# Post norms of a transformer kernel: odd feature tiles on GpSimd, all tiles singly, squares summed in the second unit

## The chip, the cores and the metric

The kernel runs on one core of a Trainium2 chip. The core has TensorE (PE, matrix products, with its weight loads as PEld), VectorE (DVE), ScalarE (ACT), GpSimd (POOL) and SyncE (SP), which issues the weight loads. Each engine works through its own instructions in order and waits on semaphores for the others. The metric is the device time of one execution in microseconds, the median of several runs. The profile is one more execution, recorded by the hardware profiler; its span is the time from its first to its last instruction.

## The reference

Two transformer blocks in fp32 on 256 tokens of width 1024; before the second block 16 learned tokens are put in front (272 tokens). The first block (sparse attention, latent attention, two MLPs) is not touched. The second one:

```python
def rmsnorm(x, g):
    y = xf * lax.rsqrt(jnp.mean(xf * xf, axis=-1, keepdims=True) + EPS)
    return y * g
for i in range(DEPTH):                                   # DEPTH = 2
    f = swiglu(rmsnorm(h, ffn_norm_pre[i, 0]), w1, w3, w2)
    h = h + 0.5 * rmsnorm(f, ffn_norm_post[i, 0])
    hn = rmsnorm(h, mix_norm_pre[i])
    m = causal_multiscale_pool(hn, ...) if i % 2 == 0 else diff_attention(hn, ...)
    h = h + rmsnorm(m, mix_norm_post[i])
    f = swiglu(rmsnorm(h, ffn_norm_pre[i, 1]), w1, w3, w2)
    h = h + 0.5 * rmsnorm(f, ffn_norm_post[i, 1])
```

So the state h is rebuilt six times as h + norm(f) * gain, and the next norm and product start from it. The change concerns five of these: those that lead into the pool mixer, ffn1, ffn2, the qkv product of the attention, and ffn3. The sixth, at the kernel's end, is done in another way.

## The kernel before, in words

Everything is kept with features on the partitions: the state `X` (`x_state`) is 8 tiles of 128 features by 272 tokens (256 in the last one), `F` (`mixer_out`) holds the output of the product before it, already times its gain. Every product is done as three products of fp32r parts: a high part (`XH`, `xg_high`, made by ScalarE as state times gain) and a low part (`XL`, `xg_low`, the rest, made by VectorE); the weights are split the same way in chunks of 128 x 2048 (`split`: ScalarE copies `w_raw` to `w_high`, VectorE subtracts into `w_low`). A large product is a sequence of units; a unit uses one chunk, 8 feature tiles, two output tiles, 3 matmuls each: 48 matmuls into one of two accumulators `acc`. Unit j needs the low part of chunk j, and that `acc` was evacuated after unit j-2. The norm's factor 1/rms is applied to the output, so unit 0 can run before the sum of squares is known.

At a seam into the next product the order is written out by hand:

- PE sums the squares of `F` over the partitions with a matrix of ones (`sum_with_last`), ScalarE takes log and exp for a first guess of 1/rms (`root`), VectorE makes the variance and three Newton steps (`variance`, `refine`, `newton`; the result is `rstd`).
- VectorE's `post_norm` multiplies `F` by `rstd` into `ta` (`evac_a`) and adds it to `X`, in groups `FINE`: tiles 0, 1, 2-3, 4-5, 6-7; behind each it makes the low parts of the group before.
- ScalarE's `xg` makes the high parts of each group and squares each pair of tiles.
- PE's `up` first runs 5 idle products of 512 columns (`keep_busy`, line 562), then unit 0, tile by tile as the groups come (`xg_waits(FINE)`), with further idle products behind tiles 0 and 1 and the squares of tiles 0 to 3 summed directly from `squares` (`sum_tiles`, line 600); VectorE folds tiles 4 to 7 into `square_sum` (`squares_after`, `fold_squares`), which PE adds behind unit 0 (`sum_rest`, line 607).
- Then ScalarE's `root` for the new norm, `rstd` again, VectorE's evacuation of unit 0 (line 1909), and the split of the third chunk on both engines. The second chunk was split before the seam (`ahead`), except for ffn1, where it is split in the seam.
- At the pool mixer PE runs four pieces of two feature tiles each instead of units, then the sum of squares per token; VectorE folds all eight squares.

GpSimd does little: two constant tables, copies of rope parts in the first block (lines 505 and 510), two tables for the last attention (lines 515 and 516).

## Time and profile before

| | us |
|---|---|
| median of 3 runs | 1645.82 |
| lowest, highest | 1645.07, 1648.28 |
| span of the profiled execution | 1639.2 |
| PE busy | 1596.5 (97%) |
| PEld busy | 1522.2 (93%) |
| VectorE busy | 1011.4 (62%) |
| ScalarE busy | 763.7 (47%) |
| GpSimd busy | 22.7 (1%) |

The profiled execution is given by its span alone; the runs' time also holds what lies around the span. Busy times are averages over the whole kernel; a busy PE includes the idle products of line 562. A timeline row has the start from the span's start, the duration, engine, line, operation, output<-input, shape, a count where several are merged, and in brackets the idle time before it and what ended it. The engines overlap the end of one operation with the start of the next one, so starts may be closer together than the durations.

### The profile page before, as it was taken

How to read it: one execution, taken by the hardware profiler on the slowest of the kernel's cores; microseconds unless marked ns; L12 is line 12 of the kernel's file. 1: busy time of each engine (PE TensorE's matmuls, PEld its weight loads, DVE VectorE, ACT ScalarE, POOL GpSimd, SP SyncE). 2: the span in 40 equal slices, each digit the busy share in tenths (PEclk: the TensorE clock that was granted, in tenths of full speed). 3: DMA queues.
4: the chain of work that ended last, by engine and by line, in shares of the span. 5: the costliest groups of instructions: out<-in, count | busy, mean ns of one | idle time of the engine just before them, and what ended most of it. 6: DMA issues, size and time to landing. Idle time of an engine off the chain costs nothing.

```text
span 1639.2 us, 31001 instructions
## 1 busy us (share of the span) xinstructions
PE 1596.5 (97%) x12665; PEld 1522.2 (93%) x12665; DVE 1011.4 (62%) x1239; ACT 763.7 (47%) x1004; POOL 22.7 (1%) x40
## 2 busy tenths in 40 slices
PE   7989999998999999999999999999999999999999
PEld 5969999998999998999978999989999898889998
DVE  7786665567666546565457665466664656676653
ACT  4345554447555435434445444344443435654443
POOL 0000000013000000000000000000000000000000
PEclk9999999999999999999999999999999999999999
DMA  6701566644266665556622556635567352246673
GB/s 165 184 27 56 180 200 182 196 142 122 78 180 197 188 185 167 176 163 198 183 77 87 174 178 200 182 103 180 179 188 194 102 184 78 78 129 190 194 212 96
DMA packets 347111, 253.03 MB, mean 154 GB/s; under 512 B 32622, under 2 KB 345868, under 8 KB 347036
## 3 DMA queue, kind: packets, MB, share of 16 engines
q1 hardware_dynamic: 345424, 250.00, 51.8%
q10 hardware_dynamic: 1612, 1.97, 0.4%
q8 instruction: 54, 0.88, 0.2%
q14 instruction: 21, 0.17, 0.0%
HBM read 250.90 MB, written 1.05 MB: 154 GB/s over the span
## 4 chain that ended last, share of the span: by engine, by line
PE 86%; DVE 8%; ACT 3%; DMA 2%; issue 1%; SPq 0%; ACTq 0%; DVEq 0%
PE acc L537 25%; PE acc L539 25%; PE acc L538 25%; DVE w_low L1682 2%; ACT w_high L1194 1%; PE acc L562 1%; PE spare L735 1%; PE acc L767 1%; DMA w_raw<-in_ffn_w_dram 1%; PE spare L562 1%; PE acc L753 1%; DVE x_state L1892 1%; DVE xg_low L1726 1%; DVE evac_a L1890 1%; PE acc L1089 1%
## 5 line engine op out<-in xcount | busy, mean ns | idle before, releaser
L1682 DVE TENSOR_TENSOR w_low<-w_raw,w_high 128x2048 fp32r<-128x2048 f32 (+2 forms) x222 | 528.7, 2381 | 379.4 <-ACT w_high L1194 379.4
L1194 ACT ACTIVATE w_high<-w_raw 128x2048 fp32r<-128x2048 f32 (+2 forms) x222 | 441.4, 1988 | 612.9 <-PE acc L539 580.2
L537 PE MATMUL acc<-xg_high,w_high 128*128 128x272 f32 (+2 forms) x2320 | 663.3, 286 | 8.1 <-DVE xg_low L1726 4.4
L538 PE MATMUL acc<-xg_low,w_high 128*128 128x272 f32 (+2 forms) x2320 | 654.6, 282 | 0.0
L539 PE MATMUL acc<-xg_high,w_low 128*128 128x272 f32 (+2 forms) x2320 | 654.6, 282 | 0.0
L537 PEld LDWEIGHTS acc<-xg_high,w_high 128*128 128x128 f32 (+1 forms) x2320 | 435.4, 188 | 20.0 <-issue 9.3
L538 PEld LDWEIGHTS acc<-xg_low,w_high 128*128 128x128 f32 (+1 forms) x2320 | 435.4, 188 | 2.4 <-issue 1.7
L539 PEld LDWEIGHTS acc<-xg_high,w_low 128*128 128x128 f32 (+1 forms) x2320 | 435.4, 188 | 0.2
L537 PE MATMUL acc<-hidden_high,w_high 128*128 128x256 f32 (+1 forms) x1216 | 342.4, 282 | 2.8 <-DVE w_low L1682 2.8
L539 PE MATMUL acc<-hidden_high,w_low 128*128 128x256 f32 (+1 forms) x1216 | 341.7, 281 | 0.0
L538 PE MATMUL acc<-hidden_low,w_high 128*128 128x256 f32 (+1 forms) x1216 | 341.7, 281 | 0.0
L537 PEld LDWEIGHTS acc<-hidden_high,w_high 128*128 128x128 f32 x1216 | 228.8, 188 | 3.8 <-DVE w_low L1682 2.0
L539 PEld LDWEIGHTS acc<-hidden_high,w_low 128*128 128x128 f32 x1216 | 228.8, 188 | 0.0
L538 PEld LDWEIGHTS acc<-hidden_low,w_high 128*128 128x128 f32 x1216 | 228.6, 188 | 0.0
L1909 DVE TENSOR_TENSOR evac_a<-acc,rstd 128x544 f32<-128x544 f32 (+1 forms) x44 | 31.5, 716 | 38.9 <-PE acc L539 38.8
L1917 DVE TENSOR_TENSOR evac_b<-acc,evac_a 128x544 f32<-128x544 f32 (+1 forms) x44 | 31.5, 716 | 35.4 <-PE acc L539 35.0
L562 PE MATMUL spare<-constants,ones 128*128 128x512 f32 (+1 forms) x120 | 49.5, 546 | 1.0 <-DMA constants<-in_constants_dram 1.0
L1199 ACT ACTIVATE xg_high<-x_state,gains 128x272 fp32r<-128x272 f32 (+1 forms) x72 | 33.6, 507 | 28.1 <-DVE x_state L1892 20.9
L562 PEld LDWEIGHTS spare<-constants,ones 128*128 128x128 f32 x120 | 22.0, 194 | 18.5 <-issue 16.4
L537 PE MATMUL acc<-out_high,w_high 128*128 128x256 f32 x128 | 36.3, 283 | 0.5 <-DVE out_low L2015 0.5
L539 PE MATMUL acc<-out_high,w_low 128*128 128x256 f32 x128 | 36.1, 282 | 0.0
L538 PE MATMUL acc<-out_low,w_high 128*128 128x256 f32 x128 | 35.7, 279 | 0.0
(296 smaller groups left out, 1448.2 us busy)
## 6 DMA issues: line engine op xcount, KB each, us to landing
w_raw<-in_ffn_w_dram SPq DMA_DIRECT2D x88, 1024.0 KB, 5.3
w_raw<-in_ffn_w_dram SPq DMA_DIRECT2D x32, 1408.0 KB, 7.0
w_raw<-in_mlp_w_up_dram SPq DMA_DIRECT2D x32, 1024.0 KB, 5.7
w_raw<-in_mlp_w_down_dram SPq DMA_DIRECT2D x32, 1024.0 KB, 5.6
w_raw<-in_attn_w_qkv_dram SPq DMA_DIRECT2D x12, 1024.0 KB, 5.1
w_raw<-in_a_w_in_dram SPq DMA_DIRECT2D x18, 256.0 KB, 4.3
w_raw<-in_a_w_in_dram SPq DMA_DIRECT2D x4, 1024.0 KB, 8.0
w_raw<-in_a_w_out_dram SPq DMA_DIRECT2D x4, 1024.0 KB, 5.1
```

The lines of the kernel that those rows point to most:

```text
L537: pe.matmul(dst, high_w, high, start=first, stop=False)
L538: pe.matmul(dst, high_w, low, start=False, stop=False)
L539: return pe.matmul(dst, low_w, high, start=False, stop=last)
L562: pe.matmul(bank[:, 0:width], ones[:], cst[:, 0:width], start=True, stop=True)
L735: ins = pe.matmul(sp[p % 2][:, c, 0:k.shape[1]], q, k, start=True, stop=not masked(p))
L753: ins = pe.transpose(acc[0][0:nk, p % 2, slot * P:(slot + 1) * P], Pr[p % 2][:, c, k0:k0 + nk], ident)
L767: ins = pe.matmul(acc[1][:, p % 2, c * w:(c + 1) * w], PT[p % 2][0:nk, slot, :], v, start=first, stop=last)
L1194: act.activation(whi[slot(c)][:, 0:SIZES[c]], raw[c % 2][:, 0:SIZES[c]], ACT.Copy).then_inc(S["w_high"], 1)
L1199: ins = act.activation(XH[:, k, 0:T], src[:, k, T0:T0 + T], ACT.Identity, scale=gain[:, gcol + k:gcol + k + 1])
L1682: dve.tensor_tensor(wlo[slot(c)][:, s], raw[c % 2][:, s], whi[slot(c)][:, s].bitcast(F32), ALU.subtract)\
L1909: dve.tensor_tensor(z, acc[(g.u0 + j) % 2][:, :, 0:T], across(rstd[:, 0:T], 2), ALU.mult)\
L1917: dve.tensor_tensor(a, acc[(g.u0 + j + 1) % 2][:, :, 0:T], q, ALU.mult).then_inc(S["dve_evac"], 1)
```

## The change

Five things are changed together, at all five seams.

1. `post_norm` goes tile by tile. VectorE multiplies and adds the even tiles 0, 2, 4, 6; GpSimd (`post_norm_odd`) multiplies and adds the odd tiles 1, 3, 5, 7, in the scratch `tb` (`evac_b`), once `rstd` is ready (`post_rstd`), and signals each with `x_pooled`. VectorE still makes all the low parts.
2. ScalarE (`xg_posted`) makes the high part of each tile singly; the squares of tiles 0-1 and 2-3 follow tiles 2 and 4, those of 4-5 and 6-7 come at the end. PE waits for every tile singly.
3. Unit 0 has no idle products between its tiles and no sums of squares. VectorE folds all eight squares by pairs (`fold_by_pairs`), and PE sums the result in the second unit, behind its second tile (`sum_in_second`). ffn0 stays as it was.
4. The third chunk is split before the root of the new norm, on ScalarE and on VectorE; before, it came after.
5. At ffn1 the second chunk's high part is copied by GpSimd, after pool's product, and VectorE subtracts it before the post norm.

```diff
+            def post_norm_odd(layer, T0, T):
+                pool.wait_ge(S["post_rstd"], layer + 1)
+                for q, k in enumerate(range(1, KD, 2)):
+                    t = tb[q % 2][:, 0, 0:T]
+                    pool.tensor_tensor(t, F[:, k, T0:T0 + T], rstd[:, 0:T], ALU.mult).then_inc(S["pool_step"], 1)
+                    pool.wait_ge(S["pool_step"], 4 * layer + q + 1)
+                    x = X[:, k, T0:T0 + T]
+                    pool.tensor_tensor(x, x, t, ALU.add).then_inc(S["x_pooled"], 1)
+            post_norm_odd(0, 0, T2)
+            c = G["ffn_up1"].c0 + 1
+            pool.wait_ge(S[f"w_landed{c % 2}"], LANDED[c])
+            pool.wait_ge(S["w_used"], c - 1)
+            pool.wait_ge(S["w_high"], c)
+            pool.tensor_copy(whi[slot(c)][:, 0:SIZES[c]], raw[c % 2][:, 0:SIZES[c]]).then_inc(S["w_high"], 1)
+            for layer in range(1, 4):
+                post_norm_odd(layer, 0, T2)
...
+            post_norm_odd(4, META, SEQ)
...
+            def sum_in_second(T):
+                def beside(k):
+                    if k == 1:
+                        sum_squares(T, 1)
+                return beside
...
-                wide(g, 0, T0, T, xg_waits(groups), beside=None if norm_sum else sum_tiles(T))
-                if norm_sum is None:
+                wide(g, 0, T0, T, xg_waits(groups), beside=sum_tiles(T) if by_tile else None)
+                if by_tile:
                     sum_rest(T)
                 begin(g)
-                wide(g, 1, T0, T, between=norm_sum)
+                wide(g, 1, T0, T, between=norm_sum, beside=None if norm_sum or by_tile else sum_in_second(T))
...
-                up(G[f"ffn_up{i}"], T0, T, FINE, KF2 // 2, 5)
+                up(G[f"ffn_up{i}"], T0, T, SINGLES if i else FINE, KF2 // 2, 5, by_tile=i == 0)
...
-                pe.wait_ge(S["xg_ready"], n.add("xg_ready", 1 if q else 2))
+                pe.wait_ge(S["xg_ready"], n.add("xg_ready", 2))
...
+            def xg_posted(gcol, T0, T):
+                for k in range(KD):
+                    sem_ = "x_pooled" if k % 2 else "x_ready"
+                    act.wait_ge(S[sem_], n.add(sem_))
+                    high_parts(k, k + 1, gcol, T0, T, X)
+                    if k in (2, 4):
+                        make_squares(k - 2, k, T0, T, D, X)
+                for k in (4, 6):
+                    make_squares(k, k + 2, T0, T, D, X)
+                n.add("squares")
...
-                    if first:
+                    if first and i == 0:
                         root(T)
                     split(g.c0 + j + 2, it, 2)
+                    if first and i:
+                        root(T)
...
             root(T2)
-            split(G["ffn_up1"].c0 + 1)
-            xg(PRE + KD, 0, T2)
+            xg_posted(PRE + KD, 0, T2)
...
+                product(0)
+                into_state(0)
+                product(2)
+                low_parts(0, 1, gcol, T0, T)
+                into_state(2)
+                low_parts(1, 2, gcol, T0, T)
+                low_parts(2, 3, gcol, T0, T)
+                for k in (4, 6):
+                    product(k)
+                    into_state(k)
+                    low_parts(k - 1, k, gcol, T0, T)
+                    low_parts(k, k + 1, gcol, T0, T)
+                low_parts(KD - 1, KD, gcol, T0, T)
+            def fold_by_pairs(T):
+                dve.wait_ge(S["sq_made"], n.add("sq_made"))
+                for a in (2, 4, 6):
+                    dve.wait_ge(S["sq_made"], n.add("sq_made"))
+                    link(dve.tensor_tensor(squares[:, 0:2, 0:T], squares[:, 0:2, 0:T], squares[:, a:a + 2, 0:T], ALU.add))
+                dve.tensor_tensor(sqsum[:, 0:T], squares[:, 0, 0:T], squares[:, 1, 0:T], ALU.add).then_inc(S["sq_read"], 1)
...
+                    if first and i:
+                        split(g.c0 + j + 2)
                     if first:
                         variance(T)
                         refine(rstd, T)
...
+            split(G["ffn_up1"].c0 + 1)
             variance(T2)
-            refine(rstd, T2)
+            refine(rstd, T2, "post_rstd")
             post_norm(0, T2, gcol=PRE + KD)
-            squares_after(G["ffn_up1"].c0 + 1, T2)
+            fold_by_pairs(T2)
```

VectorE at the seam into ffn2, from the first multiply by `rstd` to the first chunk's split in the new product, before (`evac_a` is the scratch, `w_low_54` the third chunk's low part):

```order
L1890 TENSOR_TENSOR evac_a_74<-mixer_out,rstd 128x544
L1892 TENSOR_TENSOR x_state<-x_state,evac_a_74 128x544
L1726 SCALAR_TENSOR_TENSOR xg_low<-x_state,gains,xg_high 128x272 x4
L1711 TENSOR_TENSOR squares<-squares 128x544
L1714 TENSOR_TENSOR square_sum<-squares 128x272
L1748 TENSOR_SCALAR variance<-spare 128x272
L1756 SCALAR_TENSOR_TENSOR rstd_step<-rstd_guess,variance 128x272
L1757 TENSOR_TENSOR rstd_step<-rstd_step,rstd_guess 128x272
L1758 SCALAR_TENSOR_TENSOR rstd<-rstd_step,rstd_guess 128x272
L1909 TENSOR_TENSOR evac_a_74<-acc,rstd 128x544
L1682 TENSOR_TENSOR w_low_54<-w_raw_50,w_high_52 128x2048
```

And the same place now:

```order
L1935 TENSOR_TENSOR x_state<-x_state,evac_a_75 128x272
L1768 SCALAR_TENSOR_TENSOR xg_low<-x_state,gains,xg_high 128x272 x3
L1957 TENSOR_TENSOR squares<-squares 128x544 x3
L1958 TENSOR_TENSOR square_sum<-squares 128x272
L1724 TENSOR_TENSOR w_low_54<-w_raw_50,w_high_52 128x2048
L1790 TENSOR_SCALAR variance<-spare 128x272
L1798 SCALAR_TENSOR_TENSOR rstd_step<-rstd_guess,variance 128x272
L1799 TENSOR_TENSOR rstd_step<-rstd_step,rstd_guess 128x272
L1800 SCALAR_TENSOR_TENSOR rstd<-rstd_step,rstd_guess 128x272
L1973 TENSOR_TENSOR evac_a_74<-acc,rstd 128x544
```

The fold has four additions instead of two, and the third chunk's subtraction moved from behind the evacuation to ahead of the variance.

ScalarE at the same seam, before (`w_high_52` is the third chunk's high part):

```order
L1205 ACTIVATE squares<-x_state 128x544
L1199 ACTIVATE xg_high<-x_state,gains 128x272 x2
L1205 ACTIVATE squares<-x_state 128x544
L1236 ACTIVATE rstd_guess<-spare,epsilon 128x272
L1238 ACTIVATE rstd_guess<-rstd_guess 128x272
L1194 ACTIVATE w_high_52<-w_raw_50 128x2048
```

And now:

```order
L1227 ACTIVATE xg_high<-x_state,gains 128x272 x3
L1233 ACTIVATE squares<-x_state 128x544 x2
L1222 ACTIVATE w_high_52<-w_raw_50 128x2048
L1276 ACTIVATE rstd_guess<-spare,epsilon 128x272
L1278 ACTIVATE rstd_guess<-rstd_guess 128x272
```

Two squares stand together at the end, and the third chunk moved ahead of the two steps of the root.

## Rows read from the trace of the kernel before

**Rows 1.** The page's part 4: shares of the chain by engine.

```profile
PE 86%; DVE 8%; ACT 3%; DMA 2%; issue 1%; SPq 0%; ACTq 0%; DVEq 0%
```

**Rows 2.** VectorE's timeline at ffn2's seam: start, us, what, count [idle before].

```profile
1081.99 0.44 DVE L1890 TENSOR_TENSOR evac_a<-mixer_out,rstd 128x272 f32<-128x272 f32 x1
...
1090.64 0.91 DVE L1726 SCALAR_TENSOR_TENSOR xg_low<-x_state,gains,xg_high 128x272 fp32r<-128x272 f32 x2 [0.24 <-ACT xg_high L1199]
1091.47 0.72 DVE L1711 TENSOR_TENSOR squares<-squares 128x544 f32<-128x544 f32 x1
...
1095.81 0.44 DVE L1748 TENSOR_SCALAR variance<-spare 128x272 f32<-128x272 f32 x1 [3.14 <-ACT rstd_guess L1236]
...
1097.78 0.72 DVE L1909 TENSOR_TENSOR evac_a<-acc,rstd 128x544 f32<-128x544 f32 x1
1098.42 2.28 DVE L1682 TENSOR_TENSOR w_low<-w_raw,w_high 128x2048 fp32r<-128x2048 f32 x1
```

**Rows 3.** ScalarE's timeline at the same seam.

```profile
1082.94 0.52 ACT L1199 ACTIVATE xg_high<-x_state,gains 128x272 fp32r<-128x272 f32 x1 [2.48 <-DVE x_state L1892]
...
1090.44 0.64 ACT L1205 ACTIVATE squares<-x_state 128x544 f32<-128x544 f32 x1
...
1096.14 1.90 ACT L1194 ACTIVATE w_high<-w_raw 128x2048 fp32r<-128x2048 f32 x1
```

**Rows 4.** PE there: first two rows from the chain, then its timeline.

```profile
1089.98 0.92 PE spare L600 x4
...
1094.79 0.46 PE spare L607 x2
...
1094.89 0.49 PE L537 MATMUL acc<-xg_high,w_high_ahead 128*128 128x272 f32 x1
...
1101.11 0.29 PE L537 MATMUL acc<-xg_high,w_high 128*128 128x272 f32 x1
```

**Rows 5.** GpSimd's timeline in the first block's second attention.

```profile
366.12 0.39 POOL L505 COPY b_k<-b_k 32x256 f32<-32x256 f32 x1
366.46 0.58 POOL L505 COPY b_k<-b_k 32x256 f32<-32x256 f32 x1
```

**Rows 6.** VectorE there; GpSimd's copies begin at 364.39.

```profile
363.04 0.42 DVE L1776 TENSOR_TENSOR evac_b<-evac_a,cos_b 96x256 f32<-96x256 f32 x1
...
370.32 0.61 DVE L1776 TENSOR_TENSOR evac_b<-evac_a,cos_b 128x256 f32<-128x256 f32 x1
370.85 0.41 DVE L1777 TENSOR_TENSOR evac_b<-spare,sin_b 128x256 f32<-128x256 f32 x1
```

**Rows 7.** GpSimd's timeline in the qkv product.

```profile
1305.42 2.19 POOL L515 CAST c_identity<-constants 128x128 fp32r<-128x128 f32 x1 [919.04 <-DVE c_q L2281]
1307.56 0.28 POOL L516 CAST c_mask<-constants 128x128 fp32r<-128x128 f32 x1
```

**Rows 8.** VectorE there.

```profile
1305.18 2.28 DVE L1682 TENSOR_TENSOR w_low<-w_raw,w_high 128x2048 fp32r<-128x2048 f32 x1
```

**Rows 9.** PE's timeline at pool's product: its start, and behind its end.

```profile
846.60 0.36 PE L1017 MATMUL acc<-w_high,xg_high 128*128 128x256 f32 x1 [2.33 <-DVE xg_low L1726]
...
856.37 0.72 PE L1026 MATMUL spare<-ones,square_sum 128*128 128x1 f32 x6
```

**Rows 10.** VectorE at pool's seam, and ahead of ffn1's post norm.

```profile
842.50 0.44 DVE L1890 TENSOR_TENSOR evac_a<-mixer_out,rstd 128x272 f32<-128x272 f32 x1
...
857.74 0.16 DVE L1756 SCALAR_TENSOR_TENSOR tokens_step<-tokens_guess,tokens_variance 128x3 f32<-128x3 f32 x1 [0.15 <-ACT tokens_guess L1361]
...
873.33 0.44 DVE L1748 TENSOR_SCALAR variance<-spare 128x272 f32<-128x272 f32 x1 [2.10 <-ACT rstd_guess L1236]
```

**Rows 11.** Windows: length, busy (x count) by engine, then PEclk, DMA, GB/s.

```profile
390.00:391.00 1.00, 0.00 (x0) 0.00 (x0) 1.00 (x1) 0.99 (x3) 0.00 (x0) 1.00 0.00 0
392.00:393.00 1.00, 1.00 (x6) 1.00 (x5) 0.31 (x1) 0.14 (x1) 0.00 (x0) 0.50 0.03 10
...
840.00:848.00 8.00, 5.67 (x22) 2.96 (x22) 7.13 (x15) 4.10 (x9) 0.00 (x0) 1.00 0.00 0
```

More of the change, by code:

```diff
@@ L1571, in _ @@
             root(T2)
-            split(G["ffn_up1"].c0 + 1)
-            xg(PRE + KD, 0, T2)
+            xg_posted(PRE + KD, 0, T2)
             ffn(1, 0, T2)
-            xg(PRE + 2 * KD, 0, T2)
+            xg_posted(PRE + 2 * KD, 0, T2)
             ffn(2, 0, T2)
-            xg(GAIN["mix_norm_pre_2"] + KD, 0, T2)
+            xg_posted(GAIN["mix_norm_pre_2"] + KD, 0, T2)
             g = G["qkv"]
+            split(g.c0 + 2)
             root(T2)
-            for j in range(11):
+            for j in range(1, 11):
                 split(g.c0 + j + 2)
@@ L1649, in _ @@
             root(SEQ)
[L1650 removed]
+            xg_posted(PRE + 3 * KD, META, SEQ)
             ffn(3, META, SEQ)
@@ L1910, in pair @@
                         .then_inc(S["dve_evac"], 1)
-                    split(g.c0 + j + 2, it, 2)
+                    if not first or not i:
+                        split(g.c0 + j + 2, it, 2)
                     dve.wait_ge(S["gate_silu"], at(ge0 + j // 2 + 1, it, 1))
@@ L1962, in ffn @@
                     variance(T)
-                    refine(rstd, T)
+                    refine(rstd, T, "post_rstd")
                     post_norm(T0, T, gcol=gcol)
```

46 lines of the change are left out of this document (22 added, 24 removed).

## The prediction

> **What bounds the kernel now.** I read the page's chain by engine first [rows 1]: PE holds 86% of it and VectorE 8%, so time can only be won or lost where PE waits. The change sits at five such places, the seams where a post norm rebuilds the state before the next large product: into pool, ffn1, ffn2, qkv and ffn3. I call R the start of the first multiply by the post norm's `rstd`. I took the seam into ffn2, R = 1081.99 [rows 2], as the pattern and read it engine by engine; the others have the same rows.
>
> PE begins unit 1 at 1094.89, R+12.9, and unit 2 at 1101.11: 6.2 for a unit of eight tiles, 0.78 a tile [rows 4]. Unit 0 ends at 12.9 because it holds, beside its own 6.2, two sums of two squared tiles (0.92 each) and one of `square_sum` (0.46) [rows 4], small fillers, and waits for `xg_low`. VectorE needs until 1090.64 + 0.91, R+9.5, for products, additions and low parts [rows 2]. Unit 2, at R+19.1, needs two things of VectorE: the evacuation of unit 0 (1097.78 + 0.72 = 1098.50) and the low part of its chunk (1098.42 + 2.28 = 1100.70) [rows 2]. The second comes last, with 0.3 to 0.4 to spare: unit 1 ends at that same moment. So two deadlines count, the end of unit 0 and the start of unit 2.
>
> **What a GpSimd operation costs.** No GpSimd tensor_tensor is in the trace. Nearest: a cast of 128 columns 0.28 [rows 7], a copy of 256 columns 0.39 [rows 5], so 0.17 plus 0.86 ns per column, 0.41 for 272 columns with one input. With two inputs I double the column part: 0.64. From above: the same copy beside VectorE took 0.58 [rows 5]; doubling its column part (0.41) gives 0.82 + 0.17, about 1.0. I take the middle of 0.41 and 1.0, 0.70, because it lies next to the doubled copy.
>
> **Who shares with whom.** While GpSimd copied, a VectorE multiplication with both inputs in SBUF took 0.61 where the same line took 0.42 before GpSimd had begun; the next one, with an input in PSUM, stayed at 0.41 [rows 6]. The copy itself went from 0.39 to 0.58 [rows 5]. A GpSimd cast of 128 columns that takes 0.28 alone took 2.19 when it met a VectorE subtraction of 2.28 in progress [rows 7, 8]. I read this as turns: one of them moves data, then the other. Products, additions, low parts and folds of the new seam all have two SBUF inputs, so GpSimd's work is not beside VectorE's, it alternates with it.
> The Trainium skill says this outright (SBUF — State Buffer, section Who interferes with whom): a VectorE instruction with two SBUF inputs contends with a GpSimd one that reads SBUF, and the second to issue is blocked. By that rule, the trace agrees: 2.19 against 0.28.
>
> **The change at the seam into ffn2, with turns.** A GpSimd operation and its turn of VectorE take 0.70 + 0.19 (0.58 less 0.39) = 0.89. Eight of them start at R+0.3: odd tiles are in the state at about 2.0, 3.8, 5.6 and 7.4. VectorE gets eight operations in between, the last the product of tile 4. Behind that stand in a row: addition of tile 4 (0.3 to R+7.7), its high part on ScalarE (0.52 [rows 3]), the low parts 3 and 4 (to 8.8), product and addition of tile 6 (2 x 0.44, R+9.7), high parts 6 and 7 (0.94), low part 7 (0.5): R+11.2, against 9.5 before. PE waits for each tile singly, has 0.78 per tile, and no sums in unit 0 any more (two pairs, 1.84, and the last, 0.46, are gone from it). So unit 0 ends 0.2 for PE to see the last low part and one tile (0.8) behind it, R+12.2, 0.7 earlier than before.
> That 0.7 is spent at the next deadline. Unit 1 now holds the sum (0.46): 12.2 + 6.2 + 0.46 = R+18.9. The squares of tiles 4 to 7 (0.64 each pair [rows 3]) end at R+11.9; the fold, three additions of 0.72 [rows 2] with 0.03 between and one of 0.44, ends at R+13.85, just when PE asks for it, two tiles into unit 1 (12.2 + 1.6). Unlike before, the third chunk's split stands ahead of the root: ScalarE's high part waits for unit 0's end, 12.3 + 1.90 [rows 3] = 14.2; VectorE's subtraction 2.28 to 16.6; then variance and Newton steps, 1095.81 to 1097.78, 1.97 [rows 2], and the evacuation 0.72: R+19.3, unit 2 at R+19.4. Queued behind that subtraction on VectorE is the whole root, and PE waits for it. Before: R+19.1. Loss: 0.3. Later units have slack: per pair of units, 12.4 of PE, VectorE has two subtractions of 2.28 and four operations of 0.72, 7.4.
>
> **The other seams.** qkv and ffn3 have the same order (ffn3 with 256 columns): 0.3 each. ffn1: 0.3, and one more: its second chunk's subtraction (2.28) now stands before `variance`, in an idle time of 2.10 [rows 10]: 0.2 more, 0.5. Its high part goes to GpSimd: 2048 x 0.86 ns + 0.17 = 1.9, which begins when pool's product ends.
> Pool, R = 842.50 [rows 10]: PE starts at 846.60 and works through four pieces with fillers until 856.37, 2.44 each [rows 9]; it waits only for the first. Pieces wait for pairs: low part 1 comes at R+5.0, low part 3 at R+8.1; from there 0.2 + 3 x 2.44 puts the end at R+15.6 against 13.9: 1.7. Then GpSimd's cast of 1.9 starts at the moment where VectorE's three-column Newton step stands 1.3 later [rows 10]; by turns that step waits for the rest, 0.6, and PE with it. And PE is idle before the first piece for 2.33 + (5.2 - 4.1) = 3.4 instead of 2.33 [rows 9]. At 390 to 391 PE did nothing, and at 392 the granted clock was 0.50, the 1.2 GHz level [rows 11]; a first piece (2.1 of work) at that level costs what it doubles less the 1.0 that it would wait anyway, about 1. I take 0.4, since before the 2.33 left the clock at 1.00 [rows 11]. Pool: 2.7.
>
> **Sum.** 2.7 + 0.5 + 3 x 0.3 = 4.1 us over the profiled 1639.2. That execution is given by its span alone; it lies 6.6 below the median of the runs, 1645.82, and I carry the difference over: **1649.9**. PE's clock elsewhere, the DMA queue and SP's waits are untouched: SP waits for `w_low`, which comes no later than before except by these amounts.
> At the ends of the price: with 0.41 the turns are 0.60, the last low part is at R+8.9 and unit 2 about 1.7 early at four seams: 4 x -1.7, pool -0.4, cast +0.3, ffn1 +0.2, 1639. With 1.0: +3.0 at four seams, pool +5.7: 1664.
>
> **Rivals.**
> 1. No turns worth the name (GpSimd's two-input form holds VectorE back little). Then VectorE's own 16 operations of 0.36 to 0.44 with their waits end at R+7.8, PE is bound by itself: unit 1 at R+9.1, unit 2 at R+16.2, 2.9 early at four seams, pool 1.9 early; minus 13: **1632.5**. For it: the work halves on paper. Against: [rows 6 to 8].
> 2. Turns, with a dearer operation: 0.80, still between the 0.64 and the 1.0 of the rows, gives turns of 0.99, unit 2 at +1.0 and pool at +3.4: **1653.5**. The Trainium skill (GPSIMD Engine Reference, section Elementwise — side-by-side cycle accounting) has 4497 ns for 2048 fp32 columns, 2.2 ns per column; an estimate from it is 0.77 for 272, and no run here shows it. By that figure the sum would be near this rival's.
> 3. PE's clock. Unit 0 loses its fillers; with bursts of 0.9 and waits of 0.4 to 1.5, if the level fell to 1.2 GHz at each seam as in [rows 11], a unit 0 that is half waiting loses about 1 to 2: **1657**. Decides: whether PE's rest between tiles counts as idle. Against: 2.33 of idle at pool, more than any wait here, left the level at 1.00 [rows 9, 11].
> 4. The gain of unit 0 is real but late work takes it all and no more: **1646**.
>
> **How the numbers follow.** Turns with 0.6 to 0.9: 0.50, of which 0.15 within 0.2% (3.3 us, about what a measurement of this kernel can tell) and 0.35 slower. Turns with a cheaper operation: 0.15 (faster 0.10, same 0.05). No turns: 0.18, faster. Clock: 0.07, slower. Dearer than 0.9: 0.06, slower. No effect: 0.04. Faster 0.28, same 0.24, slower 0.48. The range leaves out half of the no-turn case and the last of the dear one: 1634 to 1660.
>
> **What would show it.** GpSimd's tensor_tensor at 0.7 or more beside VectorE, and VectorE's 0.44 operations printed at 0.6 to 0.9 until R+7.4; unit 1's first matmul near R+12.3, unit 2's near R+19.4 with an idle time ended by `evac_a`. I am wrong if VectorE's operations stay at 0.44 while GpSimd works, if the first matmul of unit 1 comes before R+10.5, or if the granted clock leaves 1.00 in a unit 0.

## The result, and the profile after

| | median us | runs |
|---|---|---|
| before | 1644.71 (1638.98 to 1648.37) | 16 |
| after | 1650.53 (1643.63 to 1661.49) | 16 |

The ratio is 1.0049, 95% interval 1.0034 to 1.0064 (it is not the quotient of the two medians, which differ by 5.8 us only). 0.49% of 1644.71 is 8 us, where the prediction had 4.1 us (0.25%) and a time of 1649.9. The profiled execution of after spans 1650.7, that of before 1639.2.

The page of after, chain by engine, answers [rows 1]: PE gave two points, one to VectorE and one to ScalarE.

```profile
PE 84%; DVE 9%; ACT 4%; DMA 2%; issue 1%; SPq 0%; ACTq 0%; DVEq 0%
```

GpSimd's timeline of after at ffn2's seam (R = 1085.03 here): start, us, what [idle before]. The rows left out alternate in the same way.

```profile
1085.08 1.01 POOL L521 TENSOR_TENSOR evac_b<-mixer_out,rstd 128x272 f32<-128x272 f32 x1 [199.98 <-DVE rstd L1800]
1086.17 0.84 POOL L524 TENSOR_TENSOR x_state<-x_state,evac_b 128x272 f32<-128x272 f32 x1
...
1091.68 0.85 POOL L524 TENSOR_TENSOR x_state<-x_state,evac_b 128x272 f32<-128x272 f32 x1
```

VectorE's timeline there answers [rows 2].

```profile
1085.03 0.44 DVE L1931 TENSOR_TENSOR evac_a<-mixer_out,rstd 128x272 f32<-128x272 f32 x1
1085.51 0.88 DVE L1935 TENSOR_TENSOR x_state<-x_state,evac_a 128x272 f32<-128x272 f32 x1
1086.31 0.99 DVE L1931 TENSOR_TENSOR evac_a<-mixer_out,rstd 128x272 f32<-128x272 f32 x1
...
1094.67 0.49 DVE L1768 SCALAR_TENSOR_TENSOR xg_low<-x_state,gains,xg_high 128x272 fp32r<-128x272 f32 x1
1095.34 0.91 DVE L1768 SCALAR_TENSOR_TENSOR xg_low<-x_state,gains,xg_high 128x272 fp32r<-128x272 f32 x2 [0.18 <-ACT xg_high L1227]
...
1098.44 0.44 DVE L1958 TENSOR_TENSOR square_sum<-squares 128x272 f32<-128x272 f32 x1
1099.76 2.29 DVE L1724 TENSOR_TENSOR w_low<-w_raw,w_high 128x2048 fp32r<-128x2048 f32 x1 [0.87 <-ACT w_high L1222]
1101.97 0.43 DVE L1790 TENSOR_SCALAR variance<-spare 128x272 f32<-128x272 f32 x1
...
1103.86 0.72 DVE L1973 TENSOR_TENSOR evac_a<-acc,rstd 128x544 f32<-128x544 f32 x1
```

ScalarE's timeline there, one row of it, answers the last of [rows 3].

```profile
1097.81 1.92 ACT L1222 ACTIVATE w_high<-w_raw 128x2048 fp32r<-128x2048 f32 x1 [0.99 <-PE acc L560]
```

PE's timeline there, the first multiplies of units 1 and 2, answers the last two of [rows 4].

```profile
1097.55 0.28 PE L558 MATMUL acc<-xg_high,w_high_ahead 128*128 128x272 f32 x1
...
1104.73 0.36 PE L558 MATMUL acc<-xg_high,w_high 128*128 128x272 f32 x1 [0.55 <-DVE evac_a L1973]
```

Eight GpSimd operations of 0.84 to 1.01 take until R+7.5, and every VectorE operation beside them that was 0.44 (0.49 for a low part) is printed at 0.88 to 1.00; the first one, which GpSimd joins at its start, is still 0.44, and those that start behind R+7.5 are at 0.43 to 0.50 again. The last low part ends at 1095.34 + 0.91 = R+11.22 against R+9.56, `square_sum` at R+13.85 against R+10.67. Unit 1 nevertheless starts earlier, R+12.52 against 12.90, as it has no sums ahead of it. Unit 2 starts later, R+19.70 against 19.12, released by `evac_a`: that is the loss. Each seam by itself, from the same rows of the two traces:

| us from R, before / after | last low part | unit 1 | unit 2 | loss |
|---|---|---|---|---|
| ffn1 | 9.56 / 11.22 | 13.02 / 12.51 | 19.03 / 19.69 | 0.66 |
| ffn2 | 9.56 / 11.22 | 12.90 / 12.52 | 19.12 / 19.70 | 0.58 |
| qkv | 9.56 / 11.22 | 12.91 / 12.51 | 19.13 / 19.66 | 0.53 |
| ffn3 | 9.17 / 10.71 | 12.25 / 11.85 | 18.19 / 18.93 | 0.74 |
| pool | 9.55 / 11.22 | | product's end 13.87 / 17.75 | 3.88 |

At the pool the product of after shows two things [rows 9 to 11] did not have. PE's timeline of after, first multiply and the row behind the product, then the windows (length, busy by engine, then PEclk, DMA, GB/s):

```profile
845.44 0.55 PE L1046 MATMUL acc<-w_high,xg_high 128*128 128x256 f32 x1 [3.39 <-DVE xg_low L1768]
...
858.02 0.72 PE L1055 MATMUL spare<-ones,square_sum 128*128 128x1 f32 x6
```

```profile
840.00:848.00 8.00, 4.61 (x17) 3.16 (x16) 7.86 (x11) 2.52 (x5) 7.04 (x8) 0.80 0.00 1
848.00:856.00 8.00, 8.00 (x51) 7.04 (x51) 5.62 (x12) 5.32 (x8) 0.00 (x0) 0.78 0.01 2
```

The granted clock averages 0.80 and 0.78 over these two windows: for 6.8 us, from 0.7 before the first multiply on, it was at 0.50, the 1.2 GHz level. PE's multiplies there are printed at 0.41, where before had 0.28 behind the first one. The second thing is GpSimd's cast. GpSimd's row and VectorE's row beside it, each from its own timeline:

```profile
858.31 1.89 POOL L531 CAST w_high<-w_raw 128x2048 fp32r<-128x2048 f32 x1 [10.54 <-PE spare L1048]
```

```profile
859.39 0.82 DVE L1798 SCALAR_TENSOR_TENSOR tokens_step<-tokens_guess,tokens_variance 128x3 f32<-128x3 f32 x1 [0.15 <-ACT tokens_guess L1403]
```

The three-column step takes 0.82 where it took 0.16 [rows 10]: it ends when the cast ends (859.39 + 0.82 and 858.31 + 1.89 are both 860.2). From the pool's end to ffn1's R it is 19.58 instead of 18.92.

Sum of the seams in this execution, with the 0.66 between the pool and ffn1: 0.66 + 0.58 + 0.53 + 0.74 + 3.88 + 0.66 = 7.05. The two profiled executions differ by 11.5, though. After was 2.2 ahead when it came to the pool's R (840.27 against 842.50), before anything that was changed, and lost 7.0 more than qkv's 0.53 between the R of qkv and that of ffn3. Most of that is at the end of the last attention, where nothing was changed. Windows of after, then of before:

```profile
1408.00:1416.00 8.00, 8.00 (x26) 6.21 (x26) 3.32 (x12) 2.67 (x12) 0.00 (x0) 0.50 0.00 0
```

```profile
1408.00:1416.00 8.00, 7.49 (x45) 5.47 (x46) 5.08 (x13) 6.06 (x13) 0.00 (x0) 1.00 0.01 2
```

From qkv's R to ffn3's R after took 159.94, before 152.41, 7.5 more. It is not all clock: 0.53 is the seam of qkv, about 1.5 a slower pace of qkv's units at full clock (6.08 each instead of 5.92, see the last section), 0.7 a longer wait of PE at R-3.6 of ffn3 (1.57 instead of 0.85) for squares that ScalarE makes behind a weight split, which itself waited for its transfer. That leaves about 4.8 for the fall. Whether it is the change's is taken up in experiment 9.

### The profile page after: what moved, and what is told of

The parts are those of the page before. It is cut to its first block, busy times and chain, and to the rows that moved or that the text cites. A ratio compares the mean times of both kernels' runs of the same rounds, so it can differ in the third digit from the quotient of the medians.

```text
span 1650.7 us, 30945 instructions
## 1 busy us (share of the span) xinstructions
PE 1597.8 (97%) x12609; PEld 1522.7 (92%) x12609; DVE 1026.0 (62%) x1238; ACT 762.2 (46%) x1003; POOL 57.4 (3%) x81
## 4 chain that ended last, share of the span: by engine, by line
PE 84%; DVE 9%; ACT 4%; DMA 2%; issue 1%; SPq 0%; ACTq 0%; DVEq 0%
PE acc L558 25%; PE acc L559 24%; PE acc L560 24%; DVE w_low L1724 2%; ACT w_high L1222 2%; PE acc L583 1%; PE acc L796 1%; DVE xg_low L1768 1%; PE spare L764 1%; DVE x_state L1935 1%; DMA w_raw<-in_ffn_w_dram 1%; DVE evac_a L1931 1%; PE acc L1117 1%; PE acc L782 1%; PE acc L1068 0%
## 5 line engine op out<-in xcount | busy, mean ns | idle before, releaser
L558 PE MATMUL acc<-xg_high,w_high 128*128 128x272 f32 (+2 forms) x2320 | 664.5, 286 | 18.2 <-DVE xg_low L1768 12.4
L521 POOL TENSOR_TENSOR evac_b<-mixer_out,rstd 128x272 f32<-128x272 f32 (+1 forms) x20 | 19.2, 958 | 1013.5 <-DVE rstd L1800 1013.5
L583 PE MATMUL spare<-constants,ones 128*128 128x512 f32 (+1 forms) x96 | 43.5, 592 | 0.9 <-DMA constants<-in_constants_dram 0.9
L1768 DVE SCALAR_TENSOR_TENSOR xg_low<-x_state,gains,xg_high 128x272 fp32r<-128x272 f32 (+1 forms) x72 | 39.8, 584 | 4.6 <-ACT xg_high L1227 4.3
```

The costliest lines, as they stand in the source:

```text
L521: pool.tensor_tensor(t, F[:, k, T0:T0 + T], rstd[:, 0:T], ALU.mult).then_inc(S["pool_step"], 1)
L558: pe.matmul(dst, high_w, high, start=first, stop=False)
L583: pe.matmul(bank[:, 0:width], ones[:], cst[:, 0:width], start=True, stop=True)
L1768: ins = dve.scalar_tensor_tensor(XL[:, k, 0:T], src[:, k, T0:T0 + T], gain[:, gc:gc + 1], XH[:, k, 0:T].bitcast(F32), ALU.mult, ALU.subtract)
```

## The experiments

Beside the reading above (VectorE and GpSimd get in each other's way) stood one rival: GpSimd does relieve VectorE, and working tile by tile, or the later sum and split, is what costs. Three kernels tell these apart: GpSimd's work added to the kernel before, taken out of the changed one, and measured alone.

**1. GpSimd beside an unchanged VectorE.** To the kernel before, at each seam:

```diff
+                for q, k in enumerate(range(1, KD, 2)):
+                    t, o = tb[q % 2][:, 0, 0:T], tb[q % 2][:, 1, 0:T]
+                    pool.tensor_tensor(t, F[:, k, T0:T0 + T], rstd[:, 0:T], ALU.mult).then_inc(S["pool_step"], 1)
+                    pool.wait_ge(S["pool_step"], 4 * layer + q + 1)
+                    pool.tensor_tensor(o, F[:, k, T0:T0 + T], t, ALU.add).then_inc(S["x_pooled"], 1)
...
```

> The kernel before, whole and unchanged in its order, with eight 272-column multiplications and additions of GpSimd at each of the five seams into scratch that nobody reads; VectorE waits for their end only before the next root and the next product, long after. Theory (GpSimd's tensor_tensor and VectorE's operations with two tensor inputs take turns): VectorE's 272-column products and additions stand at 0.85 to 1.0 us instead of 0.44 while GpSimd works, the last low part comes 2 us or more after R + 9.56, and each seam loses 1.5 us or more at the start of unit 1. Rival (no turns; in the change VectorE is late because it works tile by tile and waits for GpSimd's results): VectorE's operations keep their durations, the last low part stays at R + 9.56 and the seams are unchanged within 0.1 us.

Measured: 1665.56 in its one run. VectorE at ffn2's seam (R = 1092.54), the code of [rows 2] line for line:

```profile
1092.54 0.44 DVE L1906 TENSOR_TENSOR evac_a<-mixer_out,rstd 128x272 f32<-128x272 f32 x1
1093.02 0.88 DVE L1908 TENSOR_TENSOR x_state<-x_state,evac_a 128x272 f32<-128x272 f32 x1
...
1099.92 1.29 DVE L1906 TENSOR_TENSOR evac_a<-mixer_out,rstd 128x544 f32<-128x544 f32 x1
...
1102.72 0.72 DVE L1906 TENSOR_TENSOR evac_a<-mixer_out,rstd 128x544 f32<-128x544 f32 x1
```

0.44 becomes 0.88, 0.72 becomes 1.29, and the same line is back at 0.72 once GpSimd is done (at 1100.63). At ffn1 the last low part comes at R+13.62 instead of 9.56, unit 1 at R+17.38 instead of 13.02 (a fall of the clock is in the last number, not in the low part's). So the turns are real and need neither single tiles nor a wait for GpSimd's results.

The rule of the Trainium skill that the prediction used (SBUF — State Buffer, section Who interferes with whom), that a VectorE instruction with two SBUF inputs contends with a GpSimd one that reads SBUF, holds here. That section calls the contention an exclusive lock. If the whole printed durations excluded each other, a pair would take 0.757 (experiment 3) + 0.44 = 1.20; the rows of after have a pair every 0.92 (seven pairs in 6.43). That does not refute a lock on the data alone: VectorE's part that grows with the columns is 0.28 for 272 of them (0.72 for 544 less 0.44), and 0.28 behind GpSimd's 0.757, or behind the 0.59 that is left of it without the prediction's fixed 0.17, gives 0.87 to 1.04, an estimate with 0.92 inside.

**2. GpSimd taken out of the change.** The changed kernel with all products and additions on VectorE, singly:

```diff
-            post_norm_odd(0, 0, T2)
...
-            for layer in range(1, 4):
-                post_norm_odd(layer, 0, T2)
...
-            post_norm_odd(4, META, SEQ)
...
+                for k in range(KD):
```

> The changed kernel with all sixteen products and additions of a post norm back on VectorE, one tile at a time; GpSimd keeps only the weight cast after the pool. All else as in the change (single tiles into unit 0, the sum of squares in unit 1, third chunk split first). Theory (the two engines take turns, so that GpSimd's eight operations relieve VectorE of nothing): without them VectorE's 272-column product or addition is back at about 0.44 us instead of 0.88 to 1.00, the last low part lies at R + 10.3 instead of R + 11.22, unit 1 starts at R + 11.4 to 11.6 instead of R + 12.52, unit 2 at R + 18.6 to 18.8 instead of R + 19.70, the pool's product ends at R + 13 to 14 instead of R + 17.75, and the time is 1 to 3 us under the kernel before. Rival (GpSimd does relieve VectorE, and single tiles and the later sum cost the time): the last low part comes after R + 12 and the kernel is slower than the changed one, over 1653 us.

Measured: 1641.23, ratio to before 0.9992 (0.9978 to 1.0005). VectorE at ffn2's seam, R = 1079.97:

```profile
1079.97 0.44 DVE L1926 TENSOR_TENSOR evac_a<-mixer_out,rstd 128x272 f32<-128x272 f32 x1
1080.45 0.44 DVE L1930 TENSOR_TENSOR x_state<-x_state,evac_a 128x272 f32<-128x272 f32 x1
```

The last low part is at R+10.29, unit 1 at R+11.26, unit 2 at R+18.45, the pool's end at R+13.36. VectorE alone, with twice the operations, is 0.93 sooner than with GpSimd's help. The rival falls: at unit 2 and at the pool's end single tiles, late sum and early split together gain 0.3 to 0.7 a seam on the kernel before, and GpSimd's share turns that into a loss. In the time itself the gain does not show: the interval takes in 1, and the expected 1 to 3 us under before are neither shown nor excluded. By their ratios to before, the 0.5% between this kernel and the changed one does show, and only GpSimd's share of the post norm separates them. Its cast still stands here, and with it the stretch from the pool's end to ffn1's R is 19.70.

**3. GpSimd's price alone.** Four operations on two fp32 tiles of 272 columns at the kernel's start, in the VectorE-only kernel of experiment 4:

```diff
...
+            for i in range(4):
+                pool.tensor_tensor(step[:], var[:], guess[:], ALU.mult if i % 2 else ALU.add).then_inc(S["pool_step"], 1)
+                pool.wait_ge(S["pool_step"], i + 3)
```

> The first VectorE-only version, with four products and additions of two fp32 tiles of 272 columns on GpSimd at the very start, where nothing of VectorE with two tensor inputs runs beside them; their results are not used. It measures GpSimd's own price of such an operation. The prediction took 0.70 us for the operation and 0.19 us for a turn of VectorE. Theory: about 0.75 to 0.85 us alone, so that 0.1 to 0.2 us of the 0.92 us pitch that the changed kernel shows are turns. Rival (GpSimd is as slow alone): 0.92 to 1.0 us. Rival (it is fast alone and only the turns make it slow): 0.5 us or less.

Measured, the line's own view of that kernel (duration in ns min/median/max):

```profile
L503 POOL TENSOR_TENSOR rstd_step<-variance,rstd_guess x4: 756/757/757, 1.6 to 4.1; 128x272 f32<-128x272 f32 x4
```

0.757 alone, 0.84 to 1.01 beside VectorE; the kernel's one run took 1641.47. The prediction's 0.70 was low by 0.06. The Trainium skill (GPSIMD Engine Reference, section Elementwise — side-by-side cycle accounting) has 4497 ns for 2048 fp32 columns. By proportion that is 0.60 for 272, an estimate 0.16 under the run; the 0.77 in the prediction's rival 2 comes out only with the fixed 0.17 of the copies [rows 5, 7] added, and so it agrees with 0.757.

**4. The change's other parts without GpSimd.** VectorE as before the change in its groups 0, 1, 2-3, 4-5, 6-7, high and low parts tile by tile, the sum behind tile 1 of unit 1, the third chunk split ahead of the root:

```diff
+                for a, b in FINE:
+                    act.wait_ge(S["x_ready"], n.add("x_ready"))
+                    for k in range(a, b):
+                        high_parts(k, k + 1, gcol, T0, T, X)
...
```

> No GpSimd in any post norm or weight cast. VectorE multiplies and adds as before the change, in the groups 0, 1, 2-3, 4-5, 6-7, but makes its low parts, and ScalarE its high parts, tile by tile; the sum of the squares goes behind tile 1 of unit 1, and the third chunk of ffn1 to ffn3 is split ahead of the root, as in the change. Theory (GpSimd's turns are what the change pays; its order of the sum and the split is worth having): VectorE gets through the seam by about R + 9.6, unit 1 starts at R + 10.5 to 11.0, unit 2 at R + 17.8 to 18.1 against R + 19.03 to 19.13 before, the pool's product ends no later than R + 13.9, and the time is 4 to 6 us under the kernel before. Rival (the moved sum and split are what costs): unit 2 starts at R + 19.5 or later although unit 1 starts early, and the time is that of before or above it.

Measured: 1643.92, ratio 1.0006 (0.9992 to 1.0020). Unit 1 started at R+11.12 (expected 10.5 to 11.0), unit 2 at R+18.30 (expected 17.8 to 18.1), 0.7 to 0.8 ahead of before, but the pool's product ended at R+15.39, since the clock fell there (0.79 from 840 to 848), and the time is that of before. The expected 4 to 6 us did not come. The seams show why unit 2 is late although unit 1 is not: `w_low` of the third chunk, 2.29 long, ends at R+15.6 and only then do `variance` and the Newton steps run; `evac_a` ends at R+18.2 and releases PE. The next two concern that order.

**5. One part of the change undone: the root first again** at ffn1 to ffn3.

```diff
-                    if first and i == 0:
+                    if first:
                         root(T)
                     split(g.c0 + j + 2, it, 2)
-                    if first and i:
-                        root(T)
...
```

> The changed kernel with one part undone: at ffn1, ffn2 and ffn3 the root and VectorE's Newton steps come ahead of the third chunk's split again; qkv keeps the change's order. Theory (in the changed kernel, where the sum of the squares comes late, the split ahead of the root fills a wait and unit 2 gains little by it): evacuation of unit 0 ends earlier, near R + 18.0 instead of R + 19.55, but the low parts of the third chunk then end near R + 20 and unit 2 starts at R + 19.9 to 20.3 instead of R + 19.70, so that the part is worth 0.2 to 0.6 us a seam. Rival (the split ahead of the root is one of the losses): unit 2 starts at R + 19.4 or earlier.

The lines left out do the same on VectorE. PE's timeline there at ffn2, R = 1085.28:

```profile
1105.44 0.39 PE L558 MATMUL acc<-xg_high,w_high 128*128 128x272 f32 x1 [0.99 <-DVE w_low L1722]
```

Unit 2 at R+20.16 instead of 19.70, now released by `w_low`; `evac_a` ends at R+17.90. In the changed kernel the early split is worth 0.4 to 0.5 a seam. (Its one run took 1655.46; it has 161.77 from qkv's R to ffn3's, against 152.41 before, with the slower pace of qkv's units and the longest fall at the attention's end of all.) Up to the pool this kernel is the changed one, and its execution did not lose the clock there:

```profile
847.38 0.36 PE L1046 MATMUL acc<-w_high,xg_high 128*128 128x256 f32 x1 [3.39 <-DVE xg_low L1766]
```

```profile
848.00:856.00 8.00, 7.67 (x60) 6.76 (x59) 7.47 (x14) 5.33 (x8) 1.64 (x2) 1.00 0.01 2
```

After the same idle 3.39 as in after the clock stayed at 1.00, and the pool's product ended at R+15.58 instead of 17.75.

**6. The sum behind tile 0, root first, and the pool's seam tile by tile**, on the kernel of experiment 4:

```diff
-                    if k == 1:
+                    if k == 0:
                         sum_squares(T, 1)
...
```

> The VectorE-only version (groups 0, 1, 2-3, 4-5, 6-7 for product and addition, parts tile by tile), with three places moved: the sum of the squares stands behind tile 0 of unit 1 instead of behind tile 1, the root comes ahead of the third chunk's split again, and the pool's seam alone goes tile by tile. Theory (without GpSimd unit 1 can start at R + 11.1, and unit 2 then waits for the later of PE's own 6.7 us and the low parts of its chunk, which are ready at about R + 17.8 when the split follows the root closely): unit 2 at R + 17.8 to 18.1 at ffn1, ffn2 and qkv against 19.03 to 19.13 before, the pool's product ends at R + 13.4, and the time is 4 to 5 us under the kernel before (ratio about 0.997). Rival (the third chunk's split is better ahead of the root): unit 2 at R + 18.6 or later and a time not below that of the VectorE-only version.

Measured: 1641.32, ratio 0.9982 (0.9964 to 1.0000). Some 3 us under before with an interval that ends at 1, where 4 to 5 were expected. Unit 2 at R+18.15 (expected 17.8 to 18.1), the pool's end at R+13.36. Sum and root were moved together here, and the pair is worth 0.15 at unit 2 (18.30 in experiment 4). The rows of experiment 4 have unit 2 end its wait on a split that begins with unit 0's end, whatever the sum does, so the earlier sum (0.7) should help only with the root first; that, and that the early split pays only together with a late sum, is argued from the rows, and neither was run by itself.

**7. The clock, first attempt.** The changed kernel with idle products between tiles and eleven instead of five ahead of the pool:

```diff
+                if k < 4:
+                    keep_busy(sp[0][:, 0], 2, 256)
...
-            keep_busy(sp[0][:, 0], 5)
+            keep_busy(sp[0][:, 0], 11)
```

> The changed kernel with idle products put back into unit 0: two of 256 columns behind each of tiles 0 to 3 for ffn and qkv, and eleven instead of five ahead of the pool's first product; nothing of the norms is touched. Theory (PE's granted clock falls at a seam because the multiplies of unit 0 now come too far apart, and that costs only at the pool's product): the granted clock stays at 1.00 through each unit 0, the pool's product ends at R + 15.6 to 16.0 instead of R + 17.75, the other seams are unchanged within 0.1 us, and the time is about 2 us under the changed kernel. Rival (the fall costs nothing anywhere, the pool is late because of GpSimd's cast and steps): the pool's end stays at R + 17.4 or later with the clock at 1.00.

Measured: 1657.36 (4 runs), ratio 1.0097 (1.0076 to 1.0119), slower than the changed kernel instead of faster. It tested less than it was meant to: eleven idle products ended after the first low parts were ready and pushed the first multiply from R+5.17 to R+6.36, those between tiles put unit 1 at R+13.00 instead of 12.52, and the same helper put them into the two mlp products as well, which was not intended. What it does show: the clock stayed at 1.00 at all five seams in this execution, and the pool's product then ended at R+16.51, 1.24 earlier in spite of the late start.

**8. The clock, cleanly.** Eight idle products instead of five at the pool, nothing else:

```diff
-            keep_busy(sp[0][:, 0], 5)
+            keep_busy(sp[0][:, 0], 8)
```

> The changed kernel with eight idle products instead of five ahead of the pool's first product and nothing else altered; three more take 2.6 us, less than PE's idle gap of 3.39 us there, so that the first product is not delayed as it was with eleven. Theory (the fall of PE's granted clock after that gap costs the pool 2.7 us): the clock stays at 1.00, the first product starts at R + 5.2 and the pool's product ends at R + 15.0 to 15.2 instead of 17.75; the other four seams are as in the changed kernel within 0.05 us. Rival (the fall costs little): the end stays after R + 16.5.

Measured: 1653.27 in its one run, which fell at the attention's end and took the slower pace in ffn2's up product (the last section). The pool's window in this kernel, and PE's row behind the product (R = 841.79):

```profile
840.00:848.00 8.00, 7.18 (x24) 3.52 (x23) 7.74 (x12) 2.79 (x6) 5.83 (x7) 1.00 0.00 1
```

```profile
857.37 0.72 PE L1055 MATMUL spare<-ones,square_sum 128*128 128x1 f32 x6
```

First multiply at R+5.18, end at R+15.58, clock 1.00. So of the pool's 3.88 the fall is 2.17 and the later low parts 1.71. The expectation's 15.0 to 15.2 was too early, the prediction's own 15.6 right. That the three idle products kept the clock is not shown by this, since experiment 5 kept it with five; experiment 11, the second execution with eight, kept it too.

**9. Both kernels once more.**

> The changed kernel once more, unaltered, for one look at what repeats. What comes from the engines' own durations and order must repeat within 0.05 us (last low part R + 11.22, unit 1 R + 12.51, unit 2 R + 19.7). Open: whether the granted clock falls again at the pool's product (then R + 17.7 again, otherwise R + 15.1), and whether it falls again at the end of the last attention, where the first look lost some 7 us to the kernel before.

> The kernel before once more, unaltered. The seams must repeat within 0.05 us (last low part R + 9.56, unit 2 R + 19.1, end of the pool's product R + 13.9). Open: whether the granted clock stays at 1.00 at the end of the last attention as in the first look. If it falls here too, that part of the difference between the two profiled executions (7.5 us between the seams of qkv and ffn3) is not the change's.

Measured: 1649.38 for after and 1643.47 for before, one run each. Everything that engines and order fix repeated: unit 2 at R+19.69 and 19.71, low parts at 11.21 to 11.23; of before 19.03, 19.14, 19.12 and 9.56 to 9.58. The falls did not repeat in the same places. After: again at the pool (end R+17.52), again at ffn2 without cost, none at ffn1, but one at qkv that put unit 1 at R+14.11 and cost 1.6, and none at the attention's end (155.31 between the two R). Before: this time a fall at the pool too (end R+15.48, 1.6 late), and none at the attention's end (152.33).

At the pool, over all fourteen profiled executions, the idle time ahead of the product goes with the falls, but does not decide them: up to 1.8 none in six, at 2.33 two in four (of before the second, and experiment 4), at 3.39 two in three (after twice, not experiment 5), at 5.8 in the one of experiment 1.

At the attention's end the idle time is 1.3 in each of the twelve executions of kernels with the attention as it was. A low clock stands behind it in eight, and in four (both of before, the second of after, experiment 1) not. Between the two R's the eight took 154.33 to 161.77. The three executions that have the seams of before, experiment 1 among them, all escaped it, and of the nine of kernels made from the changed one eight did not. Chance alone would divide four escapes among twelve in that way about once in fifty times, so that the fall may well be likelier with the change, though not certain (after escaped it once) and without a known reason.

The record has the mean granted clock of every run. Over the 16 runs of after it is 0.9927, over the 74 runs of before that were made beside the experiments 0.9951, over the 12 of experiment 2 0.9957. So the changed kernel does lose more clock than before, and not only in its profile. The difference, 0.0024 of 1645, is 4 us of PE's work: an estimate of the most that the falls can add.

**10. Two idle products in the attention's gap**, on the kernel of experiment 6:

```diff
+                if p + 3 == N:
+                    pe.wait_ge(S["c_probs"], p - 1)
+                    keep_busy(acc[0][:, p % 2], 2, 256)
...
```

> The VectorE-only version with the sum behind tile 0 and the root ahead of the split, unchanged at the seams, with two 256-column idle products more in the last attention, ahead of the transposes of the third piece from the end, where PE stood idle for 1.32 us and the granted clock fell right after in six of ten profiled executions. Theory (that gap lets the clock fall, and the fall costs up to 5 us between the seams of qkv and ffn3): the clock stays at 1.00 there, the interval between the two seams' R is 152.3 to 152.6 us instead of 157.1, and the median is 1 to 3 us under that version's, some 5 us under the kernel before. Rival (the fall there is chance, or the added products are in the way): the interval stays over 153.5 us or the median does not fall.

Measured: 1636.54 against 1641.48 of before, ratio **0.9959** (0.9941 to 0.9976), the fastest of all. The attention's window in experiment 6's kernel, then in this one:

```profile
1400.00:1408.00 8.00, 8.00 (x26) 6.02 (x25) 2.44 (x11) 2.67 (x12) 0.00 (x0) 0.50 0.00 0
```

```profile
1400.00:1408.00 8.00, 7.49 (x43) 5.29 (x43) 5.91 (x19) 5.01 (x18) 0.00 (x0) 1.00 0.00 0
```

Between the R of qkv and ffn3: 157.06, then 152.09. The mean granted clock of its twelve runs is 0.997, against 0.994 for experiment 6. The intervals of the two ratios touch, so how much of the gain on before is the idle products' is not sharply known.

**11. The change, whole, without the two costly falls**: the edits of experiments 8 and 10 on the changed kernel.

> The changed kernel, its seams and its GpSimd work whole, with idle products alone added in two places: three more of 512 columns ahead of the pool's first product (eight instead of five) and two of 256 columns in the last attention, in the gap of 1.32 us. Theory (the changed kernel loses 0.5 us to 0.7 us at each of four seams and 2.4 us about the pool, some 4.9 us, to the engines' own work, and the rest of its 8 us to falls of PE's granted clock at the pool and at the attention's end): with both taken away it is at most 3 to 5 us over the kernel before, ratio 1.001 to 1.003, and the profile shows the pool's end at R + 15.6, unit 2 at R + 19.7, and 152.5 to 153.5 us between the seams of qkv and ffn3. Rival (the falls are not what makes up the difference): the ratio stays at 1.005.

Measured: 1646.97, ratio 1.0020 (1.0005 to 1.0035). The pool's end is at R+15.58, unit 2 at R+19.7, 153.43 between qkv and ffn3. The interval lies almost wholly under that of the change itself (1.0034 to 1.0064), and the mean granted clock of its runs is that of before (0.9955 and 0.9953). By the two ratios 4.7 us of the 8 go with the two falls, with some 3.5 us to either side, and the edits also take away what before itself loses at these places. The profiled execution took the slower pace in ffn2's up product, 3.0 us; whether the other eleven did is not known.

## Why the prediction was right in kind and short in size

**GpSimd alternates with VectorE: right, and shown** by experiments 1 and 2. Price 0.70 against 0.757 measured, turn 0.19 against about 0.16 (pitch 0.92 less 0.757): the two errors nearly cancel, 0.89 against 0.92. Odd tiles were predicted in the state at 2.0, 3.8, 5.6 and 7.4 and came at 2.0, 3.8, 5.7 and 7.5; the last low part at R+11.2 came at 11.22, the fold's end at 13.85 to the hundredth.

**Unit 1 at R+12.2: 12.52.** The step that failed is "0.2 for PE to see the last low part and one tile (0.8) behind it". PE does not wait for the last low part. It waits for tile 5's, which ends at 1094.67 + 0.49 = R+10.13; tiles 6 and 7 are ready before PE gets to them, so three tiles of 0.74 stand behind that wait: 10.13 + 0.16 + 2.23 = 12.52 (0.16 is what is left over for seeing it and for the slower first multiply). With singly arriving tiles the deadline is the latest of (arrival + what is left), not the last arrival.

**Unit 2 at R+19.4: 19.70.** The chain was the predicted one, link by link: ScalarE's split waits for unit 0 and starts at R+12.78 instead of 12.3, VectorE's subtraction ends at 17.02 instead of 16.6, `evac_a` at 19.55 instead of 19.3, and PE's idle time is ended by it. The 0.3 comes from unit 0's end. A loss of 0.3 a seam was thus 0.53 to 0.74, at ffn3 most. ffn1's extra 0.2 for its second chunk's subtraction did not show: `variance` there comes 0.7 later after the pool's end than before, and the cast's 0.66 accounts for that. Terms of the four seams: 1.4 predicted, 2.5 measured.

**Pool: 2.7 predicted, 4.54 measured** (3.88 + 0.66). The later low parts, 1.7, were 1.71; the cast's collision, 0.6, was 0.66, and in the three kernels without GpSimd's cast (experiments 3, 4 and 6) the stretch is 18.92 as before. The term that was mis-sized is the clock: 0.4 taken, 2.17 and 1.94 measured in the two executions of after. "I take 0.4, since before the 2.33 left the clock at 1.00" is the reasoning that failed: the same 2.33 lost the clock in the second execution of before. One profiled execution showed a chance outcome, and the prediction read it as a fact. Its own estimate of 1 for a fall, from [rows 11], was half of what a fall cost. What the change adds on average is less than 2.17, as experiment 5 had no fall after the same 3.39 and before itself loses 1.6 in some executions; seven executions are too few for a number.

**Rival 3, the clock at each seam,** was given 0.07, with "Against: 2.33 of idle at pool, more than any wait here, left the level at 1.00". It happened in part. In after the clock fell in unit 0 of ffn1 and ffn2 in the first execution, of ffn2 and qkv in the second, which the prediction itself names as a sign of being wrong. Most cost nothing, because unit 0 was waiting for VectorE anyway; one cost 1.6. Rival 2 (0.80 an operation, 1653.5) was as near to the measured 0.757 as the forecast; its pitch of 0.99 was too long by 0.07. Rival 1, no turns, fell with experiment 1.

**The total.** Seams and cast without falls: 2.5 + 1.71 + 0.66 = 4.9 by this count, and experiment 11 shows 3.3 (0.8 to 5.8), with the two falls absent in its profile. The falls bring it towards the measured 8.0; the mean clocks of experiment 9 allow them up to 4. So the forecast of 4.1 was close for the engines' own part, and what it left out is the clock. That 1649.9 lies within a microsecond of the median of after, 1650.53, is partly luck: the 4.1 was added to a median of before, 1645.82, that was 1.1 above the later one, and the medians differ by less than the ratio says. The DMA queue, called untouched, may not be: PE's wait at R-3.6 of ffn3, behind a split that waits for its transfer, is 1.57 and 1.71 in the two executions of after against 0.85 and 0.78 in those of before. The reason is not shown.

## What to carry to other kernels

Work given to GpSimd does not relieve VectorE while VectorE's own instructions have two inputs in SBUF: here 0.76 and 0.44 together took 0.92 a pair, and VectorE alone was done sooner with all sixteen operations. When waits between tiles take the place of fillers, price the clock from several executions rather than from one, and fill the gap only up to the moment when the data arrives: with five idle products the pool lost 2.2 us in two executions of three, with eight nothing in two, and with eleven its start came 1.2 late. The split ahead of the root was worth 0.4 to 0.5 with a late sum, and the best kernel here has it behind, with an early sum; such parts are judged together.

## What the runs showed of the hardware

- VectorE's and GpSimd's operations both stretch when they overlap: 0.44 to 0.88 and more, 0.757 to between 0.84 and 1.01; a VectorE operation of 0.72 gains about the same half microsecond (1.29). A pair takes 0.92, less than the 1.20 of both alone. A three-column VectorE step that met a cast of 1.89 ended with the cast.
- PE's granted clock behaved differently after the same idle time in different executions: after 2.33 it stayed at 1.00 in one execution of before and fell in the next, after 3.39 it fell in two executions and stayed in a third, and after 1.3 in the attention it fell in eight of twelve.
- PE's units have two speeds at a granted clock of 1.00, in the same kernel. ScalarE's splits in the qkv product, which follow PE unit by unit, two units apart, in the first and in the second execution of after:

```profile
1324.64 1.92 ACT L1222 ACTIVATE w_high<-w_raw 128x2048 fp32r<-128x2048 f32 x1 [4.16 <-PE acc L560]
...
1336.80 1.92 ACT L1222 ACTIVATE w_high<-w_raw 128x2048 fp32r<-128x2048 f32 x1 [4.16 <-PE acc L560]
```

```profile
1321.39 1.92 ACT L1222 ACTIVATE w_high<-w_raw 128x2048 fp32r<-128x2048 f32 x1 [4.75 <-PE acc L560]
...
1333.23 1.92 ACT L1222 ACTIVATE w_high<-w_raw 128x2048 fp32r<-128x2048 f32 x1 [4.00 <-PE acc L560]
```

  6.08 against 5.92 a unit, the same code in both. Each time one whole product has the slower pace: qkv in the first execution of after and in experiment 5, ffn1's up product in experiment 1, ffn2's in experiments 4, 8 and 11, where 19 units make 3.0 us (209.09, 210.48 and 210.49 from R to R, against 206.05 for experiment 3's kernel, that of 4 at this place, and 207.45 for after). Its cause was not looked into.
